# Gather rings of five input slots and ten output slots in place of eight and eight

## What is computed

```python
q = (t @ w_pq).reshape(n, PEER_HEADS, 2, PEER_DQ // 2)
sub = jnp.einsum('nhpd,hpkd->nhpk', q, peer_keys).astype(F32)
sc, ix = lax.top_k(sub, PEER_TOPK)
...
best, pos = lax.top_k(cand, PEER_TOPK)
experts = jnp.take_along_axis(cand_ix, pos, axis=-1)
gates = jax.nn.softmax(best, axis=-1).astype(h.dtype)
...
act = jax.nn.gelu(jnp.einsum('nd,nhkd->nhk', tb, peer_u[eb]))
return jnp.einsum('nhk,nhkd->nd', gb * act, peer_v[eb])
```

## Time and profile before

| what | value |
|---|---|
| median of three runs | 5391.55 us |
| profiled execution, its own time | 5387.88 us |
| its span, first to last instruction | 5386.1 us |
| PE, DVE, POOL, ACT busy | 82%, 62%, 52%, 26% |
| row phases, first to last gather issued | 972.6 to 2663.9 us and 3643.9 to 5350.2 us |
| u gathers, v gathers | 1280 and 1280, 512 KB each |
| issue to landing of a gather, median | 11.7 us |

### The profile page before, as it was taken

How to read it: one execution, slowest core, us unless ns; L and a number is a source line. 1 busy time by engine, 2 the same in 40 slices (tenths; PEclk the granted TensorE clock), 3 DMA queues, 4 the chain that set the end, 5 groups by cost and what they waited for, 6 DMA issues and landing times. The chain is left out here.

```text
span 5386.1 us, 51105 instructions
## 1 busy us (share of the span) xinstructions
PE 4440.8 (82%) x15092; PEld 2253.3 (42%) x15092; DVE 3353.6 (62%) x8542; ACT 1396.1 (26%) x3530; POOL 2775.4 (52%) x2690
## 2 busy tenths in 40 slices
PE   8788899788878878777697888987988788887775
PEld 3488664433323323222245886643333233332222
DVE  5455474666666666766465554746666666666664
ACT  1221453222222222222202114522222222222221
POOL 0022100577777777777600220007777777777775
PEclk9888899999999999999998888998999999999999
DMA  7100001899999999999860000029999999999998
GB/s 248 39 3 1 16 1 55 331 409 409 409 405 404 404 400 398 399 398 399 351 237 13 3 1 16 1 72 378 409 409 409 406 405 403 396 403 391 386 395 317
DMA packets 425563, 1471.60 MB, mean 273 GB/s; under 512 B 46528, under 2 KB 52288, under 8 KB 424768
## 3 DMA queue, kind: packets, MB, share of 16 engines
q0 software_dynamic: 368640, 1342.34, 63.2%
q1 hardware_dynamic: 56640, 125.89, 6.6%
HBM read 1464.49 MB, written 3.57 MB: 273 GB/s over the span
## 5 line engine op out<-in xcount | busy, mean ns | idle before, releaser
L1525 PE MATMUL psall<-ring,diag 128*128 128x512 f32 x5120 | 2483.2, 614 | 674.5 <-DMA ring<-in_peer_v,eidx 555.6
L1337 DVE CUSTOM_DVE_ANT_0 ring<-ring,mixed 128x1024 f32<-128x1024 f32 x1280 | 1565.0, 1223 | 1013.8 <-DMA ring<-in_peer_u,eidx 1013.3
L1256 POOL DMA_INDIRECT ring<-in_peer_u,eidx x1280 | 1285.1, 1004 | 1136.8 <-DVE eidx L1194 747.0
L1525 PEld LDWEIGHTS psall<-ring,diag 128*128 128x128 f32 x5120 | 888.1, 190 | 2225.2 <-DMA ring<-in_peer_v,eidx 1472.8
L1256 POOL DMA_INDIRECT ring<-in_peer_v,eidx x1280 | 1313.6, 1026 | 411.9 <-issue 262.8
L1422 ACT ACTIVATE act<-dot 128x2 f32<-128x2 f32 x640 | 130.2, 203 | 2269.7 <-DVE dot L1337 2269.7
L1414 ACT ACTIVATE diag<-cons,wgt 128x128 f32<-128x128 f32 x1280 | 443.1, 393 | 209.6 <-DVE wgt L1317 207.5
L464 POOL TENSOR_TENSOR mlt<-lt,lmask 128x512 f32<-128x512 f32 x120 | 174.5, 1464 | 471.2 <-DVE lt L550 333.1
L1481 PE MATMUL psall<-h2T,wq 128*128 128x128 f32 (+1 forms) x1024 | 285.9, 434 | 1.3 <-DVE x L1299 1.3
L456 POOL MEMSET state<- 64x512 f32 x2 | 1.0, 518 | 502.0 <-POOLq L375 502.0
L1481 PEld LDWEIGHTS psall<-h2T,wq 128*128 128x128 f32 x1024 | 157.7, 191 | 132.4 <-issue 130.7
(11 more groups left out here) (285 smaller groups left out, 4851.0 us busy)
## 6 DMA issues: line engine op xcount, KB each, us to landing
mixed<-in_w_mod SPq DMA_DIRECT2D x32, 1024.0 KB, 5.4
wq<-in_w_pq SPq DMA_DIRECT2D x64, 512.0 KB, 6.8
ring<-in_peer_u,eidx POOLq DMA_INDIRECT x1280, 11.7
ring<-in_peer_v,eidx POOLq DMA_INDIRECT x1280, 11.7
wring<-in_w_mod SPq DMA_DIRECT2D x8, 2048.0 KB, 14.4
wring<-in_w_in_tm SPq DMA_DIRECT2D x4, 2048.0 KB, 12.5
ring<-in_w_out SPq DMA_DIRECT2D x4, 2048.0 KB, 11.4
wring<-in_w_in_fm SPq DMA_DIRECT2D x2, 2048.0 KB, 8.4
```

Source lines behind the costliest of these rows:

```text
L1256: nc.gpsimd.indirect_dma_start(out=ring[:, n % slots, :], out_offset=None, in_=d[table], in_offset=bass.IndirectOffsetOnAxis(ap=p.eidx[:, ...
L1337: nc.vector.tensor_tensor_reduce(out=p.u[:, n % UR, :], in0=p.u[:, n % UR, :], in1=p.mixed[:, t, :], scale=1.0, scalar=0.0, op0=ALU.mult, ...
L1525: mm = nc.tensor.matmul(bank, p.diag[:, n % VR, :], p.v[:, n % VR, 512 * c:512 * c + 512], start=(s == 0), stop=(s == UNIT - 1))
```

## The change

The u ring gets five slots in place of eight, the v ring ten in place of eight. The ring tensor shrinks from 16 to 15 slots of 4 KB per partition; the pieces of it that hold other things before the row phase keep their places. The diagonal matrices follow the v ring, with ten slots; the earlier use of their first eight is kept. The distance at which v gathers follow u gathers is four rows before and after.

```diff
-UR = VR = 8
+UR, VR = 5, 10
 LAG = 4
...
             p.diag = sb(c1, "diag", [P, VR, P])
-            p.diag4 = p.diag[:, :, :].rearrange("p (b k) n -> p b (k n)", b=2)
+            p.diag4 = p.diag[:, 0:8, :].rearrange("p (b k) n -> p b (k n)", b=2)
```

## The result

The changed kernel takes **5426.41 us** (median of nine runs) against 5392.58 us of the kernel before (nine runs). The medians differ by 33.8 us, the means by 28.6; the ratio, 1.0053 with an interval of 1.0033 to 1.0073, goes with the means. The prediction was +13.6 us. The direction is right and the time lies inside the range, near its upper end; the size is half of what came, or less.

A forecast was written before the change was run, and what follows sets the result against it. Gathers bound the row phase, DMA engines and POOL's issue within 3% of each other. Lost lead 5.6, longer tail 8 and v slots 0 sum to 13.6 us, giving 5405 us on the median; range 5381 to 5430.

The forecast's parts named there:

- The bound: Row phase: DMA engines full early at 409 GB/s; late, POOL's descriptors come too late; the two paces within 3%.
- Part 1: Row phases: five u slots cap issue-to-landing time at 10.3 us, not 13.1; 2.8 us lost per layer, 5.6 us together.
- Part 2: End of each layer's row phase: longer tail without lead, a bad phase repeats; 7.0 us layer 0, 1 layer 1, 8 together.
- most: Upper bound for the longer tail without lead, from soon after 1990 us in layer 0 and late layer 1; together 25 us.
- Part 3: Row phases: ten v slots and ten diagonals save at most 6.5 us per layer, all early and hidden; taken as zero.
- The tail does not notice: Rival, chance 0.36: at the layers' ends no bad phase is added; 0 to 8 us, 5392 to 5400 us.
- Faster through a better phase: Rival, chance 0.09: gathers fall between dots into the tail; 12 us gained in layer 1's last three stretches, 5380 us.
- Starved early: Rival, chance 0.05: VectorE late beyond 5 us of spare queue, early stretches slow; +110 us, 5500 us.
- The change does less than it says: Rival held likely, no separate chance: the v ring never fills its ten slots; inside the sum with zero.

The follow-up runs named there:

- half-dot kernels: Each dot over only the first 512 of 1024 columns, with eight u and eight v slots or five and ten; each 0.9962 of the kernel before.
- The second trace: The kernel before traced once more with nothing changed; 5400.97 us, one run.
- the first experiment: Five u slots but still eight v slots and eight diagonals, ring tensor kept at 15 slots; 1.0043 of the kernel before.
- split dots: Kernel before with each dot done as two 512-column instructions, sums added by ScalarE in the GELU, nothing left out; ratio 1.0007.
- weight-ring control: Kernel before with three slots instead of four in the query projection's weight ring, nothing else; ratio 1.0003.

## Why the prediction was half right

**The bound: right.** Over gathers 128 to 768 eight, six and five slots take the same 848 to 850 us by the starts and 844 to 847 by the landings. The half-dot kernels, where POOL has pace to spare, land them in 845 as well: in this piece the transfers set the pace, as the prediction had it for the early stretches, and the lead hides what POOL is late.

**Part 1, the lost lead: right in kind, too small.** The cap of 10.3 us was measured as 10.5, and the rate early was still 408. Priced at 2.8 us in a layer, it came to 4.8 + 0.5 = 5.3 by the starts. About 2.6 of this is the lead itself (13.1 - 10.5), which the landings show falling due only after gather 768, as the prediction said. The prediction looked for the rest in steady waits, "many of them", and held those hidden; there are few. It passed over the start: with no dot done yet, the sixth u gather waits 3.12 us at once, and some 2 us of landings stay lost from there on.

**Part 2, the longer tail: right in kind, wrong for layer 1, and partly lucky for layer 0.** Landing times at the floor and 126 gathers from 1996 us are what it named as the signs. With 170 / 63 = 2.698 us a row against 170 / 65 = 2.615 the price is 0.083 us a row, where 0.073 was taken. For layer 0 the term was 7.0 us, and a layer lost 4.9 + 2.7 = 7.6. But the 7.0 was reckoned over the last 500 us, where only the unsettled 2.7 lies; the 4.9 came in the 170 us ahead of them, which the prediction held only in its "most", and the phase then eased. For layer 1 the term was 1 us, and the same 7.6 came. **That is the step that failed:** from one trace, whose second layer ended badly, I took layer 1 to be in its tail already, with little left to lose. The second trace has it the other way round (516.9 and 508.5 for layer 1's last 383 gathers, 502.0 and 514.6 for layer 0's): the end of a layer varies between executions, and both layers of the changed kernel lose alike at gathers 768 to 896, which ran in 168.9 or 169.0 us in every layer of eight and eight. With 2 x 5.3 + 2 x 7.6 = 25.8 the same sum comes within the interval. Of the 12 us that the prediction lacks, 2 x 2.5 = 5 are part 1's and 15.2 - 8 = 7 part 2's.

**Part 3, ten v slots: right** beside five u slots, as the first experiment and POOL's waits show. The waits for TensorE are gone with eight v slots too (five and eight: 130.9 us over 429 times, the gap alone), so it is the u slots that take them away. It isn't a rule: beside eight u slots they give 0.3%.

**The rivals.** *The tail does not notice* falls with the third piece. The figure of the Trainium skill on which it could lean (DMA: Bandwidth & Descriptors, "Anatomy of one DMA — SWDGE (gpsimd) path", an estimate of 3.2 us) isn't met here: in the kernel before and the changed one no gather of a layer's last 512 lands in under 5.2 us. *Faster through a better phase* did not come with five slots, and did with six. *Starved early*: the second stretch fell to 404 GB/s and the third to 399, under the 405 that I had named as the point where the sum is wrong altogether. It wasn't: gathers 128 to 768 took as long as before, and the kernel before has 404 in its third stretch too. With four slots, 404 early did come with a loss in the middle, 10 to 13 us a layer. *The change does less than it says*: the ten v slots indeed never fill.

**What holds a gather** is shown in the strict sense for its size: shorter dots shorten it (968 ns against 1004), and split dots cut each hold at the end of the half. The Trainium skill (SBUF — State Buffer, "Who interferes with whom") has VectorE instructions with two SBUF inputs and GpSimd instructions that read SBUF exclude each other; the traces of half and split dots agree. The kernel before has a control for it once in 32 rows, when `add_unit` runs on VectorE:

```profile
1345.80 0.68 DVE L1329 TENSOR_TENSOR junk<-psall,gt 128x512 f32<-128x512 f32 x1
1345.99 0.94 POOL L1256 DMA_INDIRECT ring<-in_peer_v,eidx  x1 [0.30 <-issue]
...
1346.52 1.22 DVE L1331 TENSOR_TENSOR x<-x,junk 128x1024 f32<-128x1024 f32 x1
...
1347.24 1.31 POOL L1256 DMA_INDIRECT ring<-in_peer_u,eidx  x1 [0.31 <-issue]
...
1347.66 1.22 DVE L1337 CUSTOM_DVE_ANT_0 ring<-ring,mixed 128x1024 f32<-128x1024 f32 x1
```

The product of line 1329 reads one input from PSUM, and the gather that begins inside it takes its 0.94 us; the sum of line 1331 has both inputs in SBUF, and the gather that begins inside it takes 1.31, until 0.81 us after its end. So it goes all through this trace: 36 gathers begin well inside each of the two, with medians of 0.937 and 1.316 us, and 38 inside a MAX8 (line 1167, one input) with 0.937. It isn't a busy VectorE that holds a gather, then, but one with two inputs from SBUF. The other way round no lasting hold is seen: 1195 of the 1280 dots begin while a gather is running, as the last line does here, and take 1.222 us where the others take 1.230.

**Not settled:** outside the row phases the changed kernel's trace is some 13 us longer than the first trace of before. Its first gather is issued at 978.6 us (972.6 there), but at 977.9 in the second trace of before; 985.4 us lie between its row phases (980.0), but 985.8 in the weight-ring control with eight and eight. Both levels occur without the change, so I don't count them to it.

## What to carry to other kernels

When the engine that issues transfers and the transfers themselves have nearly the same pace, queue depth is a stock that is filled early and spent later: size the ring so that its slots cover the landing time at full rate plus the consumer's time and lateness (four and five u slots followed that sum here), and follow the issue-to-landing time through the phase, stretch by stretch, to see when it reaches its floor. A smaller ring then costs twice: the stock that it lacks, and what goes wrong while there is none. It costs next to nothing where the issuing engine has pace to spare. Don't read the state of a phase's end from one execution; take a second trace before a term rests on it.

## What the runs showed of the hardware

A gather that begins inside a dot runs until about 0.81 us after that dot's end, or takes its 0.935 us if that is longer; this fits 2515 of the 2560 gathers of the kernel before to 0.05 us, and most of the others begin inside the sum of line 1331, which holds them alike. A product with one input from PSUM, and a MAX8, hold no gather. Cutting the dot in two does not lessen the sum of the holds (213 us, where eight and eight have 206 and 221 in two traces). And fewer slots can be faster: six u slots gave 0.9982 and 0.9976 of the time of eight, with 0.995 us for a gather in place of 1.005 in the stretch from 1990 us.
